# Wide products for query, key, gate and branch panels in a two-layer float32 kernel, exponentials in two parts, an earlier root table, fewer issues for the last stores

## The reference

```
h = rms_norm(x)
q, k, v, forget, pin, gates = split(h @ w_in)          # q, k: 1024 wide each; gates: 2 x 2048
attn = softmax(q k / sqrt(128) + forget decays) v       # 8 heads of 128, causal
pool = multiscale_pool(pin)
merged = sigmoid(gates[0]) * (attn @ w_branch_attn) + sigmoid(gates[1]) * (pool @ w_branch_pool)
x = x + merged @ w_out
x = x + peer(rms_norm(x))     # top-16 of 16384 experts per head and token, gathered rows of two tables
```

## Time and profile before

| | |
|---|---|
| median of 3 runs (2949.0 to 2950.76) | 2949.52 us |
| profiled execution | 2951.41 us |
| its span, first to last instruction | 2949.4 us |
| TensorE busy | 2745.2 us (93%) |
| VectorE busy | 1884.3 us (64%) |
| ScalarE busy | 1297.3 us (44%) |
| GpSimd busy | 673.8 us (23%) |
| mean granted TensorE clock | 0.948 of 2.4 GHz |

### The profile page before, as it was taken

One profiled execution on the slowest core, in us unless ns is written; L12 is line 12 of the kernel. 1 busy time (PEld: TensorE's weight loads), 2 busy tenths in 40 slices (PEclk: granted clock), 3 DMA queues, 4 the chain that ended last, 5 costly groups with the idle time before them and its releaser, 6 DMA issues.

```text
span 2949.4 us, 47049 instructions
## 1 busy us (share of the span) xinstructions
PE 2745.2 (93%) x18181; PEld 2074.5 (70%) x18181; DVE 1884.3 (64%) x3070; ACT 1297.3 (44%) x2464; POOL 673.8 (23%) x576
## 2 busy tenths in 40 slices
PE   8999899999999997999999999999997887888885
PEld 8996688888888887989999889777764432222221
DVE  7885565566556565455444558899968875555556
ACT  5556443333333344435333444566565532333223
POOL 0000000000000000040000003544446675555554
PEclk9999999999999998999999999999987678999986
DMA  6443545555555553444455657999999999999998
GB/s 257 177 163 126 205 172 187 190 191 186 185 186 191 192 185 123 164 146 143 172 185 185 242 200 275 384 407 406 412 382 421 403 409 423 422 421 421 417 419 345
DMA packets 132742, 790.38 MB, mean 268 GB/s; under 512 B 34918, under 2 KB 34918, under 8 KB 37286
## 3 DMA queue, kind: packets, MB, share of 16 engines
q1 hardware_dynamic: 55184, 393.16, 36.4%
q0 software_dynamic: 77008, 394.46, 33.0%
q10 hardware_dynamic: 384, 0.52, 0.0%
HBM read 944.95 MB, written 4.19 MB: 322 GB/s over the span
## 4 chain that ended last, share of the span: by engine, by line
PE 69%; DMA 19%; DVE 6%; issue 3%; ACT 2%; POOL 1%; POOLq 0%; DVEq 0%; ACTq 0%
PE bank L2098 12%; PE bank L2099 12%; PE bank L2100 12%; PE bank L2104 10%; DMA s_u<-in_expert_u,s_u_index 9%; PE bank L2551 9%; DMA s_v<-in_expert_v,s_v_index 8%; PE bank L2105 5%; PE bank L2606 4%; PE bank L2586 1%; DVE s_w_lo L1309 1%; DMA s_raw<-in_dense_u 1%; DVE s_u L1954 1%; DVE s_yrow L1635 1%; PE bank L2205 1%
## 5 line engine op out<-in xcount | busy, mean ns | idle before, releaser
L1309 DVE TENSOR_TENSOR s_w_lo<-s_raw,s_w_hi 128x2048 fp32r<-128x2048 f32 x288 | 661.0, 2296 | 589.8 <-ACT s_w_hi L711 589.2
L711 ACT ACTIVATE s_w_hi<-s_raw 128x2048 fp32r<-128x2048 f32 x284 | 543.9, 1915 | 802.1 <-PE bank L2100 526.8
L2104 PE MATMUL bank<-s_a,s_w_hi 128*128 128x512 f32 x1408 | 493.7, 394 | 3.3 <-DVE s_w_lo L1309 3.2
L2098 PE MATMUL bank<-s_a,s_w_hi 128*128 128x256 f32 (+1 forms) x1632 | 465.5, 285 | 5.2 <-DVE s_w_lo L1309 2.9
L2100 PE MATMUL bank<-s_a,s_w_lo 128*128 128x256 f32 (+1 forms) x1632 | 463.2, 284 | 0.0
L2099 PE MATMUL bank<-s_a,s_w_hi 128*128 128x256 f32 (+1 forms) x1632 | 462.8, 284 | 0.0
L1954 DVE CUSTOM_DVE_ANT_0 s_u<-s_u,s_xn_late 128x1024 f32<-128x1024 f32 x256 | 303.7, 1224 | 222.9 <-DMA s_u<-in_expert_u,s_u_index 222.6
L2606 PE MATMUL bank<-s_v,s_spread 128*32 128x512 f32 x2048 | 307.1, 717 | 142.4 <-DMA s_v<-in_expert_v,s_v_index 116.3
L2105 PE MATMUL bank<-s_a,s_w_lo 128*128 128x256 f32 x1408 | 394.8, 280 | 0.0
L687 POOL DMA_INDIRECT s_v<-in_expert_v,s_v_index x256 | 317.7, 1241 | 272.0 <-PE bank L2606 207.4
L667 POOL DMA_INDIRECT s_u<-in_expert_u,s_u_index x256 | 301.5, 1178 | 300.1 <-DVE s_halfdot L1954 143.4
(11 more groups left out here) (361 smaller groups left out, 3402.1 us busy)
## 6 DMA issues: line engine op xcount, KB each, us to landing
s_raw<-in_stream SPq DMA_DIRECT2D x292, 1024.0 KB, 4.8
s_raw<-in_expert_v SPq DMA_DIRECT2D x40, 1024.0 KB, 8.8
s_raw<-in_dense_u SPq DMA_DIRECT2D x37, 1024.0 KB, 8.9
s_tap_blocks<-in_taps POOLq DMA_DIRECT2D x9, 512.0 KB, 3.7
s_u<-in_expert_u,s_u_index POOLq DMA_INDIRECT x256, 19.9
s_v<-in_expert_v,s_v_index POOLq DMA_INDIRECT x256, 21.4
s_panel_early<-in_dense_u POOLq DMA_DIRECT2D x3, 1024.0 KB, 10.4
s_xres<-in_x SPq DMA_DIRECT2D x2, 1024.0 KB, 5.7
```

The lines of the kernel that those rows point to most:

```text
L711: act.activation(w_hi[s % 2][:, :], raw[s][:, :], ACT.Copy).then_inc(hi_ready, 1)
L1309: dve.tensor_tensor(w_lo[s % 2][:, :], raw[s][:, :], w_hi[s % 2][:, :].bitcast(f32), ALU.subtract)\
L2098: pe.matmul(dst, left[0], right[0], start=start, stop=False)
L2104: pe.matmul(dst, left[0], both, start=start, stop=False)
```

## The change

- Query, key, gate and branch panels get the wide form. VectorE adds the two halves: for query, key and gates in a new `halves_out` at the end of a round's low parts, with ScalarE's sigmoid afterwards in place; in the branches by `tile_added` into a new buffer `whole`, ahead of each multiply. The operands of the branches are laid so that both parts can be reached in one pattern.
- ScalarE prepares the next stage's first high part before the sigmoids of a stage, not behind them.
- The exponentials are done in two halves with the third high part between them; VectorE's third low part stands before the softmax's division; the first gates' sigmoids stand behind both pooled halves.
- The root table is loaded three high parts earlier in the last ffn round.
- For the last 128 rows' stores, SP and ScalarE issue one DMA per quarter each, for 64 KB x 2.

```diff
@@ buffers
+    at_both = place("s_at", [128, 2, HEADS, T], S + 61 * K, f32r)
+    at_hi, at_lo = at_both[:, 0], at_both[:, 1]
...
+    po_span = place("s_po", [128, 37, T], S + 24 * K, f32r)
+    po_hi, po_lo = po_span[:, 0:8], po_span[:, 29:37]
+    whole = place("s_whole", [128, 8, T], S + 41 * K)
...
+        def two_chunks(q, c):
+            return out[128 + q * Q:128 + (q + 1) * Q, c * 512:(c + 2) * 512].rearrange("p (c n) -> c p n", c=2)
@@ SP, last 128 rows; ScalarE the same with two_chunks(q, 2)
+                        sp.dma_start(two_chunks(q, 0), out_row[0:2 * Q, t, q * 512:(q + 1) * 512]).then_inc(stored, 16)
@@ ScalarE, ffn
                 split_hi(8)
                 hidden_hi(1)
+                if last:
+                    early_root()
                 for c in range(9, 12):
                     split_hi(c)
@@ ScalarE, qk
-                    copies_out(i, qk, 0)
@@ ScalarE, gates; gates_1 likewise
                 for j in range(4):
-                    if j < 3:
-                        act.wait_ge(bank_full[j], n.after(f"full{j}", 1))
-                    else:
-                        act.wait_ge(panel_used, n.after("used", 4))
-                    act.activation(merged[:, bass.ds(i * 4 + j, 1), :].rearrange("p a t -> p (a t)"), bank[j][:, 0:T], ACT.Sigmoid)\
-                        .then_inc(bank_empty[j], 1)
+                    act.wait_ge(bank_empty[j], n.after(f"empty{j}", 1))
+                    mine = merged[:, bass.ds(i * 4 + j, 1), :].rearrange("p a t -> p (a t)")
+                    act.activation(mine, mine, ACT.Sigmoid).then_inc(sig_ready, 1)
@@ ScalarE, first gates
-                    exponentials()
-                    split_hi(2)
+                    with n.rounds(act, "softmax"):
+                        act.wait_ge(negmax_ready, n.after("negmax", 1))
+                        exponentials(range(4))
+                        split_hi(2)
+                        exponentials(range(4, HEADS)).then_inc(exp_ready, 1)
                     pooled(0)
                     split_hi(3)
+                    pooled(1)
                     gates_0(0)
-                    pooled(1)
@@ ScalarE, merge: gates_0 does split_hi 0 to 4, gates_1 and branches 1 to 4 and 1 to 3
                 with n.rounds(act, "gates_0"):
-                    for c in range(4):
+                    for c in range(5):
                         split_hi(c)
                     gates_0(i)
@@ VectorE
+            def halves_out(dst, first):
+                for j in range(4):
+                    if j < 3:
+                        dve.wait_ge(bank_full[first + j], n.after(f"full{first + j}", 1))
+                    else:
+                        dve.wait_ge(panel_used, n.after("used", 4))
+                    dve.tensor_reduce(dst(j), bank[first + j][:, :].rearrange("p (h t) -> p t h", h=2), AX.X, ALU.add)\
+                        .then_inc(bank_empty[first + j], 1)
@@ VectorE, at the end of each round of qk, gates_0, gates_1
+                    halves_out(lambda j: qk[:, 4 * i + j, :], 0)
@@ VectorE, branches; the second half likewise with gate1 and banks 4 to 7
+                def tile_added(b):
+                    dve.tensor_reduce(whole[:, b, :], bank[b][:, :].rearrange("p (h t) -> p t h", h=2), AX.X, ALU.add)\
+                        .then_inc(bank_empty[b], 1)
...
-                    dve.wait_ge(bank_empty[j], n.after(f"empty{j}", 0))
-                    dve.tensor_tensor(merged_tile(j), merged_tile(j), bank[j][:, 0:T], ALU.mult).then_inc(bank_empty[j], 1)
+                    tile_added(j)
+                    dve.wait_ge(sig_ready, n.after("sig", j - 7))
+                    dve.wait_ge(bank_empty[j], n.after(f"empty{j}", 1))
+                    dve.tensor_tensor(merged_tile(j), merged_tile(j), whole[:, j, :], ALU.mult).then_inc(weighed_ready, 1)
@@ VectorE, first gates
                     split_lo(0)
                     split_lo(1)
+                    split_lo(2)
                     with n.rounds(dve, "softmax"):
...
-                    split_lo(2)
                     pooled(0)
                     split_lo(3)
+                    halves_out(lambda j: merged[:, j, :], 0)
                     pooled(1)
@@ TensorE
+            def gates_0(*only):
+                feature_major((0, 1, 2, 3), both_tokens, 0, 4, 4, 0, only=only, double=True)
             def gates_1(only=None):
-                feature_major((4, 5, 6, 7), tokens, 0, 4, 4, 0, only=only)
+                feature_major((4, 5, 6, 7), both_tokens, 0, 4, 4, 0, only=only, double=True)
             def branches():
-                feature_major((0, 1, 2, 3), lambda k: (at_hi[:, k, :], at_lo[:, k, :]), 0, 2, 4, 0)
-                feature_major((4, 5, 6, 7), lambda k: (po_hi[:, k, :], po_lo[:, k, :]), 2, 2, 4, 0)
+                feature_major((0, 1, 2, 3), lambda k: at_both[:, :, k, :], 0, 2, 4, 0, double=True)
+                feature_major((4, 5, 6, 7), lambda k: po_span[:, k:k + 30:29, :], 2, 2, 4, 0, double=True)
```

More of the change, by code:

```diff
@@ L109 @@
     "heads": per_round(evac=2, full=each(range(4)), empty=each(range(4))),
[L110 to L113, removed]
+    "merge": per_round(used=12, sig=8, weighed=8, part=4, full=each((0, 1, 2, 4, 5, 6), 2), empty=each(BANKS8, 2)),
+    "gates_0": per_round(used=4, sig=4, full=each((0, 1, 2)), empty=each(range(4))),
+    "gates_1": per_round(used=4, sig=4, full=each((4, 5, 6)), empty=each(range(4, 8))),
+    "branches": per_round(used=4, part=4, weighed=8, full=each((0, 1, 2, 4, 5, 6)), empty=each(BANKS8)),
     "merged": per_round(merged_hi=4, act=4),
@@ L548, in _ @@
                     sp.wait_ge(out_ready, 4 * t + q + 1)
[L549 to L552, removed]
+                    if t == 0:
+                        for c in range(4):
+                            sp.dma_start(out[q * Q:(q + 1) * Q, c * 512:(c + 1) * 512],
+                                         out_row[c * Q:(c + 1) * Q, t, q * 512:(q + 1) * 512]).then_inc(stored, 16)
+                    else:
+                        sp.dma_start(two_chunks(q, 0), out_row[0:2 * Q, t, q * 512:(q + 1) * 512]).then_inc(stored, 16)
+            sp.wait_ge(stored, 16 * (16 + 8))
         @block.gpsimd
@@ L898, in hidden_hi, with ffn @@
                     act.activation(h_hi[:, f, :], hf[:, f, :], ACT.Copy).then_inc(hhi_ready, 1)
-            def ffn(first):
+            def ffn(first, last=False):
                 for blk in range(2):
@@ L923, in _ @@
             with n.rounds(act, "ffn"):
-                ffn(False)
-                early_root()
+                ffn(False, True)
                 for b in range(8):
@@ L1001, in _, with exponentials @@
             n.past("score", HEADS // 2)
[L1003 to L1012, removed]
+            def exponentials(heads):
+                for h in heads:
+                    act.activation(lg0[:, h, :], lg0[:, h, :], ACT.Exp, bias=negmax[:, h:h + 1],
+                                   accum_out=den[:, h:h + 1])
+                    ins = act.activation(lg1[:, h, :], lg1[:, h, :], ACT.Exp, bias=negmax[:, HEADS + h:HEADS + h + 1],
+                                         accum_out=den[:, HEADS + h:HEADS + h + 1])
+                return ins
             def pooled(half):
@@ L1023, in gates_0 @@
                 for j in range(4):
-                    if j < 3:
-                        act.wait_ge(bank_full[j], n.after(f"full{j}", 1))
-                    else:
-                        act.wait_ge(panel_used, n.after("used", 4))
-                    act.activation(merged[:, bass.ds(i * 4 + j, 1), :].rearrange("p a t -> p (a t)"), bank[j][:, 0:T], ACT.Sigmoid)\
-                        .then_inc(bank_empty[j], 1)
+                    act.wait_ge(bank_empty[j], n.after(f"empty{j}", 1))
+                    mine = merged[:, bass.ds(i * 4 + j, 1), :].rearrange("p a t -> p (a t)")
+                    act.activation(mine, mine, ACT.Sigmoid).then_inc(sig_ready, 1)
             def gates_1():
-                wait(act, part_ready, n.after("part", 0))
                 for j in range(4):
[L1035 to L1040, removed]
+                    act.wait_ge(bank_empty[4 + j], n.after(f"empty{4 + j}", 1))
+                    act.activation(gate1[:, j, :], gate1[:, j, :], ACT.Sigmoid).then_inc(sig_ready, 1)
             with n.rounds(act, "gates_0"):
@@ L1063, in _ @@
                             act.activation(at_hi[:, 2 * r + e, :], bank[2 + e][:, 0:T], ACT.Copy).then_inc(evac_hi, 1)
+                split_hi(4)
                 gates_1()
             with n.rounds(act, "branches"):
-                for c in range(4):
+                for c in range(1, 4):
                     split_hi(c)
@@ L1074, in merge @@
                 with n.rounds(act, "gates_1"):
-                    for c in range(4):
+                    for c in range(1, 5):
                         split_hi(c)
@@ L1089, in _ @@
             with n.rounds(act, "branches"):
-                for c in range(4):
+                merged_split(0)
```

(13 more changed lines are left out.)

32 lines of the change are left out of this document (16 added, 16 removed).

## The result

The changed kernel takes 2969.56 us at the median of four runs, the kernel before 2949.91: a ratio of 1.0064, 95% interval [1.0052, 1.0076]. I had forecast 2946.4 and given 0.10 to "slower". The profiled execution took 2972.12 us, span 2970.2.

The account below looks back on a forecast made before the run. TensorE's panel matmuls were taken to bound the kernel; -7.4 - 1.6 - 0.35 - 0.7 + 7.0 = -3.05 us from the median 2949.52 gave 2946.4 us, range 2940.5 to 2953.8.

Parts of the forecast that it names:

- Last stores: Kernel end: one issue per queue and quarter starts the last issue 1.1 us sooner, less 0.4 for more bytes; -0.7 us.
- C: Branch rounds: a tile costs more than 1.06 us, 3 us or more idle in every half; 2956.6 us, chance 0.10.
- The sign that I had named: Kernel end: the last store issue starts at the last copy's end.
- Products: Query, key, gate and branch panels: two matmuls instead of three per product; -7.4 us, bounds 0 and -9.
- Rival D: Wide panels: the wide product saves nothing here, panels keep the narrow pace; 2953.8 us, chance 0.12.
- Stalls in the branch rounds: Branch rounds: TensorE waits for VectorE's low part behind tiles of 1.06 us each; +7.0 us.
- Rival B: Branch rounds: VectorE is in time, tiles overlap more, stalls 1 us or none; 2940.5 us, chance 0.21.
- S: Branch rounds: chained VectorE waits are free, a tile is 0.61 + 0.34, stalls 4.7 us; 2944.1 us, chance 0.12.
- Exponentials: Panel 3 of the first gates: splitting them after four of eight heads removes TensorE's idle time; -1.6 us.
- Root table: Last ffn round: earlier table load starts the squares 1.0 us earlier, TensorE losing 0.4; -0.35 us, bounds -0.7 and +0.4.
- Sum without the stores: Whole kernel: all predicted terms together except the one for the last stores; -2.35 us.

Follow-up runs that it names:

- experiment 1: Changed kernel with the last stores of the kernel before (four issues per quarter, 32 rows by 512 columns); 2950.45 us, ratio 0.9996.
- experiment 2: Kernel before with only the new last stores; 2969.37 us, ratio 1.0058.
- experiment 8: Changed kernel, old last stores, urgent low parts before fourth tiles, merged splits moved, second output panel's high and low parts before merged's last split; 2941.75 us.
- experiment 5: Kernel of experiment 1 with only the branch panels narrow again, a tile one multiply out of the bank; 2944.74 us, ratio 0.9977.
- experiment 6: Kernel of experiment 1 with each branch-round multiply one reduction later, same instructions; 2947.75 us, ratio 0.9988.
- experiment 7: Kernel of experiment 1 with exponentials in one part and the root table late again; 2953.30 us, ratio 1.0007.

## Why the prediction was wrong

- **Last stores, -0.7 with bounds 0 ("bytes bind") and -1.1: this step failed.** It is +18 to +19 instead (2969.56 - 2950.45 = 19.1 against experiment 1; experiment 2 alone: 2969.37 - 2950.99 = 18.4). I counted issues and bytes and took it for given that a store of 64 partitions is spread as one of 32 was. No row of before showed a store with another outermost dimension, so the far bound should have been worked out from the number of engines: 512 packets on two engines instead of 16. No rival held it either; C was on the right side by luck, for another reason, and its mark (3 us in every half round) didn't come. The sign that I had named, the last issue at the last copy's end, did come (2949.1 and 2949.04), and it saved nothing.
- **Products, -7.4: held**, about -7.1. TensorE's path can be read from two low parts on VectorE, one in the last ffn round ahead of everything that was changed, and the last one ahead of the second normalisation; in the kernel before, the changed kernel and experiment 8:
```profile
1080.54 2.29 DVE L1309 TENSOR_TENSOR s_w_lo<-s_raw,s_w_hi 128x2048 fp32r<-128x2048 f32 x1 [3.29 <-ACT s_w_hi L711]
...
1719.51 2.29 DVE L1309 TENSOR_TENSOR s_w_lo<-s_raw,s_w_hi 128x2048 fp32r<-128x2048 f32 x1 [3.27 <-ACT s_w_hi L711]
```
```profile
1080.73 2.29 DVE L1311 TENSOR_TENSOR s_w_lo<-s_raw,s_w_hi 128x2048 fp32r<-128x2048 f32 x1 [3.29 <-ACT s_w_hi L720]
...
1718.84 2.29 DVE L1311 TENSOR_TENSOR s_w_lo<-s_raw,s_w_hi 128x2048 fp32r<-128x2048 f32 x1 [3.27 <-ACT s_w_hi L720]
```
```profile
1080.80 2.29 DVE L1306 TENSOR_TENSOR s_w_lo<-s_raw,s_w_hi 128x2048 fp32r<-128x2048 f32 x1 [3.29 <-ACT s_w_hi L713]
...
1710.64 2.29 DVE L1306 TENSOR_TENSOR s_w_lo<-s_raw,s_w_hi 128x2048 fp32r<-128x2048 f32 x1 [3.27 <-ACT s_w_hi L713]
```
  These are 638.97, 638.11 and 629.84 us. Experiment 8, which has no stall, is 9.1 ahead; without the exponentials and the root table (below) 6.9 to 7.2 are left for the products. The round shown in experiment 5 gives 0.096 a gate panel (predicted 0.095) and 0.205 a branch panel (0.175), but not every round does as well: experiment 5 has 632.67 on this path, so the 16 branch panels save 2.8 in all, 0.18 each, as predicted. Query and key, for which I had no row, save 1.38 in 16 panels, 0.086 each. Rival D falls.
- **Stalls in the branch rounds, +7.0: held**, 7.3 of standing still. Places and releasers were as said. A tile took 1.13 instead of 1.06. I had taken 0.03 from the end of an instruction to the one that waits for it; behind a reduction, which is shorter and reads the bank, it is 0.11. Rival B falls, and S too: only without the wait (experiment 6) does a tile take the 0.95 that S gave it with the wait. On the path above the changed kernel loses 8.3 against experiment 8, 1.0 more than the standing still. About half of that is the restart: the first matmul behind a stall is followed after 0.34 us where 0.23 is usual. Where the rest goes is open. What I had no term for either is the clock behind the longest stall.
- **Exponentials, -1.6: held**, 1.8 by the idle time that came back in experiment 7, 2.1 by its low parts against those of experiment 1. The sigmoids behind the pooled halves held up nothing.
- **Root table, -0.35: of the right sign**, -0.14. In the changed kernel TensorE's wait for the transposes fell from 16.52 to 15.75, but 0.5 us came back earlier, at the panel behind the late high part (0.4 predicted). From the low part at 1080.54 to the first one behind the ffn it is 38.11 to 38.13 us in the three executions with the late table and 37.97 to 38.01 in the seven with the early one.
- **Sum without the stores:** predicted -2.35. The changed kernel is 0.9 ahead on the path above (638.11 against 638.97): 9.1 won, 8.3 given back. Experiment 1, whose profile has the drop of the clock, is 0.4 behind (639.34). Its median is -0.5, interval -3.8 to +1.5 by its ratio. Two slips in the prediction's own figures change nothing: S's four tiles are 0.44 less, not 0.46 (4.24 against 4 x 0.95), and 2949.52 - 3.05 is 2946.5.

The trade of the change is thus: 9 us won on TensorE's path, 8 given back by VectorE's order, 18 to 19 lost by the stores' shape. That comes to 17.5 to 18.2 where 19.7 was measured, with an interval of 15 to 22; the scatter of the expert stage is enough for the rest. Both losses are mendable, as experiment 8 shows.

## What to carry to other kernels

Read a DMA's access pattern from outside inwards before counting its issues: with an outermost dimension of 2 these stores had two engines, and at the end of a kernel nothing hides that. When an edit moves work to an engine that is half idle, ask where in its order the new work stands: what the next panel needs must go ahead of what nobody waits for. The wide branch panels paid only with that.

## What the runs showed of the hardware that I had not expected

- Stores with 2 outermost steps ran at 50 GB/s (DMA share 0.13), with 4 at 97 (0.26), with 32 at 272 (0.94). The two forms with fewer and larger issues made the wait at the end 10 and 19 us longer. A form with the 32 rows outermost and one issue for two chunks was not tried, so what fewer issues alone are worth stays open.
- A VectorE wait on the instruction just before cost 0.19 us (0.79 against 0.60 from start to start), although the records show no more than 0.11 between the two.
- After 2.3 us without a matmul the granted clock fell to 0.50 for 3.2 us (experiment 1; 0.79 over 8 us) in two executions of four with that wait; after stalls of up to 1.8 us in the branch rounds it didn't.
